# Both key tiles of the first block multiplied together, chunk by chunk, in the opening of a two-block transformer kernel

## The reference, cut to what matters

```python
h = rms_norm(x, swa_norm)                      # per row: x * rsqrt(mean(x*x) + 1e-6) * gain
q, k, v, gate = split(h @ w_in, [2048, 2304, 2560])   # q 2048 wide, k 256, v 256, gate 2048
k = rms_norm(k.reshape(seq, 4, 64), k_gain)    # each of the 4 key heads normalised over its 64 values
v = v.reshape(seq, 4, 64)
...
# sliding-window attention of 32 query heads over the 4 key/value heads, with a bias by distance
# and a sink; gate with silu; output projection; residual. Then a second block with 16 meta tokens.
```

## Time and profile before

| | us |
|---|---|
| median of 3 runs | 1802.08 (1800.97 to 1802.23) |
| the profiled execution's own time | 1800.38 |
| its span | 1798.7 |
| PE busy (matmul) | 1758.5, 98% |
| DVE busy | 1066.0, 59% |
| ACT busy | 912.5, 51% |

### The profile page before, as it was taken

One profiled execution on the slowest core, in us unless ns is written; L12 is line 12 of the kernel. 1 busy time (PEld: TensorE's weight loads), 2 busy tenths in 40 slices (PEclk: granted clock), 3 DMA queues, 4 the chain that ended last, 5 costly groups with the idle time before them and its releaser, 6 DMA issues.

```text
span 1798.7 us, 28913 instructions
## 1 busy us (share of the span) xinstructions
PE 1758.5 (98%) x10281; PEld 1525.7 (85%) x10281; DVE 1066.0 (59%) x2443; ACT 912.5 (51%) x2010; POOL 54.1 (3%) x81
## 2 busy tenths in 40 slices
PE   6999999999999999999999999999999999989899
PEld 5788888888877888898888988889888898877898
DVE  5466767676675334565645546465564655666876
ACT  4466656666574224444545455454544545454443
POOL 1000000000001000000000000000000000000000
PEclk9999999999999999999999999999999999999999
DMA  6433333333325444331322222222222222223441
GB/s 196 126 92 107 98 94 106 92 98 100 91 82 139 135 134 129 103 91 52 95 83 73 82 68 80 84 66 82 72 83 82 73 82 73 79 75 108 159 149 53
DMA packets 283942, 173.85 MB, mean 97 GB/s; under 512 B 16176, under 2 KB 272368, under 8 KB 283840
## 3 DMA queue, kind: packets, MB, share of 16 engines
q1 hardware_dynamic: 267136, 151.08, 28.8%
q0 software_dynamic: 15632, 20.56, 4.9%
q10 hardware_dynamic: 1088, 1.08, 0.3%
HBM read 156.86 MB, written 14.66 MB: 95 GB/s over the span
## 4 chain that ended last, share of the span: by engine, by line
PE 77%; DVE 9%; ACT 6%; issue 3%; ACTq 2%; DMA 1%; DVEq 0%; SPq 0%
PE G L640 63%; PE G L935 3%; ACTq L1506 2%; PE S L1021 1%; DVE wsum L2342 1%; ACT wh L1186 1%; PE O L1039 1%; DVE wl L2350 1%; DVE wl L1741 1%; PE G L752 1%; DMA raw<-in_swa_w_in 1%; PE S L742 1%; PE G L766 1%; PE S L741 1%; ACT wh L1695 1%
## 5 line engine op out<-in xcount | busy, mean ns | idle before, releaser
L640 PE MATMUL G<-xh,wh 128*128 128x512 f32 (+1 forms) x2432 | 792.1, 360 | 3.9 <-DVE xl L1758 2.0
L640 PE MATMUL G<-xl,wh 128*128 128x512 f32 (+1 forms) x2432 | 765.4, 349 | 0.0
L640 PE MATMUL G<-xh,wl 128*128 128x512 f32 (+1 forms) x2432 | 763.0, 348 | 0.0
L640 PEld LDWEIGHTS G<-xh,wh 128*128 128x128 f32 x2432 | 426.6, 189 | 64.9 <-issue 4.8
L640 PEld LDWEIGHTS G<-xh,wl 128*128 128x128 f32 x2432 | 423.6, 188 | 60.9
L640 PEld LDWEIGHTS G<-xl,wh 128*128 128x128 f32 x2432 | 423.9, 188 | 51.2 <-issue 2.6
L1741 DVE TENSOR_TENSOR wl<-raw,wh 128x512 fp32r<-128x512 f32 x472 | 319.4, 688 | 248.4 <-ACT wh L1186 246.0
L1186 ACT ACTIVATE wh<-raw 128x512 fp32r<-128x512 f32 x472 | 284.1, 620 | 16.5 <-PE G L640 8.2
L1563 ACT ACTIVATE att<-att,st 128x144 f32<-128x144 f32 (+3 forms) x64 | 36.9, 577 | 119.8 <-DVE wmeta L2195 68.5
L1289 ACT ACTIVATE p<-S,rq 128x256 f32<-128x256 f32 (+1 forms) x128 | 50.1, 444 | 44.7 <-PE S L742 43.2
L1299 ACT ACTIVATE p<-p,st 128x257 f32<-128x257 f32 (+1 forms) x128 | 60.6, 482 | 0.0
(11 more groups left out here) (316 smaller groups left out, 2312.6 us busy)
## 6 DMA issues: line engine op xcount, KB each, us to landing
raw<-in_w_in SPq DMA_DIRECT2D x112, 512.0 KB, 4.0
raw<-in_swa_w_in SPq DMA_DIRECT2D x68, 512.0 KB, 8.8
raw<-in_swa_w_out SPq DMA_DIRECT2D x32, 512.0 KB, 4.3
raw<-in_w_in POOLq DMA_DIRECT2D x8, 1024.0 KB, 8.1
raw<-in_w_out SPq DMA_DIRECT2D x6, 1024.0 KB, 6.9
spare<-in_w_out SPq DMA_DIRECT2D x6, 1024.0 KB, 6.5
rel_rows<-mixed POOLq DMA_DIRECT2D x16, 383.0 KB, 19.5
mixed<-in_x SPq DMA_DIRECT2D x4, 1024.0 KB, 13.5
```

Of the source, the lines that this page charges most:

```text
L640: mm = pe.matmul(d, w[:, slot, k, :], v[:, k, a:b], start=(first and n == 0), stop=(last and n == 2))
```

## The change

The two key tiles are multiplied together: for each chunk, three matmuls for tile 0 and three for tile 1. The row factors are placed after chunk 13 of both tiles. ACT and DVE split a quarter of both tiles' weights before the four chunks of x of that quarter. The high parts of the first value tile's weights are copied by ACT right after the exponential of the row factors, a quarter at a time as the key tiles leave the buffer (new semaphore `keys_done`). Both key norm chains run beside the first value tile: the key statistics stand after its chunks 5 and 13. The first value tile's load waits for four quarters of low parts, which are now quarters 0 and 1 of both key tiles. Two pairs of semaphores are merged.

```diff
@@ SP: value_weights @@
-                sp.wait_ge(w_lo, 4 + 2 * (g - 1))
+                sp.wait_ge(w_lo, 4 * (g - 1))
@@ PE @@
+            def key_tiles():
+                for k in range(KC):
+                    next_chunk(k)
+                    for g in range(KV // 2):
+                        if k % QTR == 0:
+                            pe.wait_ge(w_lo, 2 * (k // QTR) + g + 1)
+                        product([G[:, g, :]], g, k, PLAIN, k == 0, k == KC - 1, keys_done if g else None)
+                    if k == KC - 3:
+                        first_factors()
...
-            for g in range(KV):
+            key_tiles()
+            for g in range(KV // 2, KV):
                 def at_point(p, g=g):
-                    if g == 1 and p == 3:
-                        first_factors()
-                    if 0 < g <= KV // 2 and p == 5:
-                        key_stat(g - 1)
-                    if g > KV // 2 and p == 5:
+                    if g == KV // 2 and p in (2, 6):
+                        key_stat(p // 4)
+                    if g > KV // 2 and p == 3:
                         value_transpose(g - 1)
-                if g == 1:
-                    pe.wait_ge(x_lo, KC)
-                gemm(T_KV + g, g % 2, [G[:, g, :]], PLAIN, at_point, next_chunk if g == 0 else None)
+                if g == KV - 1:
+                    pe.wait_ge(kv_act, 2)
+                gemm(T_KV + g, g % 2, [G[:, g, :]], PLAIN, at_point)
@@ ACT @@
             for quarter in range(4):
                 key_split_weights(0, quarter)
+                key_split_weights(1, quarter)
...
-            key_split_weights(1, 0)
-            key_split_weights(1, 1)
             row_sum(0)
-            key_split_weights(1, 2)
             act.wait_ge(sq_act, 1)
             row_sum(1)
-            key_split_weights(1, 3)
...
+            def first_value_split(quarter):
+                if quarter == 0:
+                    act.wait_ge(raw_in[0], 16)
+                if quarter < 3:
+                    act.wait_ge(keys_done, QTR * quarter + QTR)
+                else:
+                    act.wait_ge(tile_done, 1)
+                q = slice(QTR * quarter, QTR * quarter + QTR)
+                A(wh[:, 0, q, :], raw[:, 0, q, :], ACT.Copy).then_inc(w_hi, 1)
+            for quarter in range(3):
+                first_value_split(quarter)
+            act.wait_ge(first_mm, 2)
             A(rs1[:, :], O[:, :], ACT.Copy).then_inc(rs1_ok, 1)
+            first_value_split(3)
...
-            for g in range(1, KV):
+            for g in range(KV // 2, KV):
                 for m in range(POINTS):
-                    if m == 4 and g <= KV // 2:
-                        key_square(g - 1)
-                    if m == 6 and g <= KV // 2:
-                        key_rstd(g - 1)
+                    if g == KV // 2 and m in (1, 5):
+                        key_square(m // 4)
+                    if g == KV // 2 and m in (3, 7):
+                        key_rstd(m // 4)
+                    if (g, m) in ((KV // 2, 4), (KV - 1, 0)):
+                        key_split(g - KV // 2)
                     if m % 2 == 0:
                         split((g + 1) // 2, (g + 1) % 2, m // 2, kv_loaded(g + 1))
-                    if m == 7:
-                        key_split(g - 1) if g <= KV // 2 else value_high(0)
+                    if g == KV - 1 and m == 4:
+                        value_high(0)
@@ DVE @@
             for quarter in range(4):
                 key_split_weights(0, quarter)
+                key_split_weights(1, quarter)
                 for c in range(4 * quarter, 4 * quarter + 4):
                     x_lo_of(c)
-            key_split_weights(1, 0)
-            key_split_weights(1, 1)
             row_sum(2)
-            key_split_weights(1, 2)
             dve.wait_ge(sq_dve, 1)
             row_sum(3)
-            key_split_weights(1, 3)
...
-            for g in range(1, KV):
+            for quarter in range(4):
+                split(1, 0, quarter)
+            for g in range(KV // 2, KV):
                 for m in range(POINTS):
-                    if m == 3:
-                        kv_evict(g - 1)
-                    if m == 7:
-                        if g <= KV // 2:
-                            key_finish(g - 1)
-                            key_split(g - 1)
-                        else:
-                            value_rows(0)
+                    if (g, m) == (KV // 2, 0):
+                        kv_evict(0)
+                    if (g, m) == (KV // 2, 4):
+                        key_finish(0)
+                        kv_evict(1)
+                        key_split(0)
+                    if (g, m) == (KV - 1, 0):
+                        key_finish(1)
+                        kv_evict(2)
+                        key_split(1)
+                    if (g, m) == (KV - 1, 5):
+                        value_rows(0)
                     if m % 2 == 0:
                         split((g + 1) // 2, (g + 1) % 2, m // 2)
```

More of the change, by code:

```diff
@@ L239, in build @@
         w_hi, w_lo, tile_done = sem("w_hi"), sem("w_lo"), sem("tile_done")
-        sq_act, sq_dve, rs_done, diag_ok, rs1_mm, rs1_ok = (
-            sem(n) for n in ("sq_act", "sq_dve", "rs_done", "diag_ok", "rs1_mm", "rs1_ok"))
-        gain_in, gain_t, gain_ok = sem("gain_in"), sem("gain_t"), sem("gain_ok")
+        sq_act, sq_dve, rs_done, diag_ok, rs1_ok = (
+            sem(n) for n in ("sq_act", "sq_dve", "rs_done", "diag_ok", "rs1_ok"))
+        gain_in, first_mm, gain_ok = sem("gain_in"), sem("first_mm"), sem("gain_ok")
         t_done, x_hi, x_lo = sem("t_done"), sem("x_hi"), sem("x_lo")
@@ L284, in build @@
         t_sum, s_sum = sem("t_sum"), sem("s_sum")
+        keys_done = sem("keys_done")
         df_hi, df_lo = sem("df_hi"), sem("df_lo")
@@ L680, in _ @@
             pe.wait_ge(gain_in, 16 * 2)
-            pe.transpose(T[:, 0:2 * KC], gain_rows, ident[0:2 * KC, 0:2 * KC]).then_inc(gain_t, 1)
+            pe.transpose(T[:, 0:2 * KC], gain_rows, ident[0:2 * KC, 0:2 * KC]).then_inc(first_mm, 1)
             for c in range(4):
@@ L690, in first_factors @@
                     mm = pe.matmul(O[:, P * t:P * t + P], ones, diag[:, t, :], start=True, stop=True)
-                mm.then_inc(rs1_mm, 1)
+                mm.then_inc(first_mm, 1)
                 pe.wait_ge(gain_ok, 1)
@@ L1220, in _ @@
             A(rstd[:, 0, 0:NB], rstd[:, 0, 0:NB], ACT.Exp, scale=-0.5).then_inc(rs_done, 1)
-            act.wait_ge(rs1_mm, 1)
+            def first_value_split(quarter):
[10 more added lines that the diff above has]
+            act.wait_ge(first_mm, 2)
             A(rs1[:, :], O[:, :], ACT.Copy).then_inc(rs1_ok, 1)
+            first_value_split(3)
             def key_square(c):
@@ L1760, in x_lo_of @@
                                        op1=ALU.subtract).then_inc(x_lo, 1)
-            dve.wait_ge(gain_t, 1)
+            dve.wait_ge(first_mm, 1)
             V.tensor_copy(gnorm[:, :, :].rearrange("p n c -> p (n c)"), T[:, 0:2 * KC]).then_inc(gain_ok, 1)
             def key_split_weights(g, quarter):
-                dve.wait_ge(w_hi, 4 * g + quarter + 1)
+                dve.wait_ge(w_hi, 2 * quarter + g + 1)
                 q = slice(QTR * quarter, QTR * quarter + QTR)
```

## The result

| | before | changed |
|---|---|---|
| median of 6 runs | 1802.15 us | 1808.89 us (1805.65 to 1809.58) |
| ratio | | 1.0034, 95% interval 1.0023 to 1.0045 |
| profiled execution, its own time | 1800.38 us | 1805.65 us |
| its span | 1798.7 us | 1804.0 us |

The change made the kernel 6.7 us (0.34%) slower; between the two profiled executions it is 5.3 us. The trace is of the fastest of the six executions.

The account below looks back on a forecast made before the run. PE, busy 98% of the span, was taken to bound the kernel; -0.7 + 3.85 + 2.0 + 0.3 = +5.45 us gave a forecast median of 1807.5 us, own range 1806.2 to 1809.0, wider range 1804.6 to 1810.2.

Parts of the forecast that it names:

- The hole: PE's 4.2 us wait for the second load: chunk 0's three extra matmuls fit inside it, -0.7 us.
- The chunks: Key-tile chunks: PE takes 1.84 us per chunk instead of 1.14, work moved forward, and PE still sets the pace.
- Rival A: Key-tile chunks supplied, not paced by PE; period grows to less than 1.84 us; 1801.2 us at unchanged period; 5%.
- The wait for the row factors: After chunk 13 of both key tiles: PE stands 5.0 us for the factors against 1.15, +3.85 us.
- The clock behind it: After the row-factor wait: the granted clock falls and slows the following work, +2.0 us, bounds 0 and 2.9.
- The clock in the opening: Behind the wait for the second load: the lower clock until 20.1 us stays as before, no change counted.
- Rival C: Chunk 0's extra work in the hole holds the clock up, shrinking the loss by 1.35 us: 1806.1 us; 7%.
- The key norms: Over the first value tile: PE waits 0.7 us at the second key statistic, +0.3 us net, bounds -0.4 and +2.0.
- The loads, POOL and SP: Value-tile load issued at about 19.3, bias write and unit loads later but with time in hand: 0 us.
- Rival B: Behind the row-factor wait the clock stays up over the 5.0 us: +3.45 us, 1805.5 us; 10%.
- E: Rival: no effect, the lost time is slack somewhere later in the kernel: 1802.1 us; 5%.
- D: Rival: dearer, the clock costs 2.9 us and the key norm chain 2.0: +8.0 us, 1810.1 us; 8%.

Follow-up runs that it names:

- late: Changed kernel with the row factors placed after chunk 15 of the key tiles instead of chunk 13: 1806.76 us, ratio 1.0024.
- early: Changed kernel with row sums, logarithm, exponential and diagonal matrices put among the x chunks on ACT and DVE: 1799.80 us, ratio 0.9991.
- one-number kernels: Kernel before the change, with the row factors after chunk 1 of tile 1 instead of chunk 7: 1809.04 us, ratio 1.0039.
- The kernel with the filled wait: Changed kernel with 20 extra matmuls, results unused, on PE just ahead of the row-factor wait: 1805.38 us, ratio 1.0018.
- the second trace: Changed kernel unaltered, executed and traced again on another chip: 1807.93 us, where the kernel before took 1802.48 us once.
- third trace: Changed kernel unaltered, executed and traced once more on that other chip: 1807.19 us, where the kernel before took 1802.48 us once.
- The trace with the hole filled and the row sums early: Changed kernel with row sums among the x chunks, plus transposes two chunks ahead instead of three: 1797.07 us, ratio 0.9975.

## Why the prediction was right

The forecast was 1807.5 us, the result 1808.89, inside the range. Term by term, against the profiled execution:

- **The hole, -0.7 us.** Right in kind. The six matmuls of chunk 0 ran from 13.42 to 16.15, inside the wait, and the load's landing at 17.4 did not move. They began 1.15 us later than chunk 0 before (12.27), not 0.6; the hole covers that too.
- **The chunks.** Period 1.83 us (28.70 to 37.88 is five of them, 1.84 each), forecast 1.84. Rival A is excluded: PE sets the pace.
- **The wait for the row factors, +3.85 us.** The main term, and right: PE came 40.93 - 37.72 = 3.2 us after the start of chunk 15's transposes (forecast 3.2), the factors 45.95 - 37.72 = 8.2 us after it (forecast 8.2). The late, early and one-number kernels each moved this wait as the account says.
- **The clock behind it, +2.0 us.** The term that was mis-sized. It was 3.7 us in the trace: the factor matmuls took 49.38 - 45.95 = 3.4 instead of 1.84 us, and until 54.0 each matmul took 0.427 instead of 0.232 us, some 2.1 us more. In all three traces of the changed kernel the low clock lasted 10.2 us, and only the first 0.9 to 2.2 us of it fell into the wait, where it is free. Both stretches I had drawn on were shorter, 6.8 us in all, and in the first of them 4.1 us lay in the wait. The kernel with the filled wait puts the price at 3.5 us by the medians and 3.7 by the traces. I took the middle of two rows and gave a price above the larger of them, 2.9, no room. Why it was 10.2 us here and 6.8 behind the 5.2 us wait made in the kernel before stays open.
- **The clock in the opening, 0.** I let the low clock behind the load stay. In the profiled execution it was gone, worth 1.1 us (chunk 15's transposes came at 37.72, not 38.9); in the second trace it was there and longer. Rival C's event so came about in the traced execution, but the extra work alone does not decide it: with the same six matmuls in the hole, two of the seven such traces have the higher clock at 18.5 us and five the lower until 20.5 to 22.7.
- **The key norms, +0.3 us.** Forecast a wait of 0.7 for the second statistic, found 0.63 by starts (65.60 - 64.97) against 0.28 before: +0.35. The chain from 58.55 to 65.60 is 7.05 us, forecast 7.0 to 7.1.
- **The loads, POOL and SP, 0.** The value tile's load was issued at 19.44 (forecast 19.3), and no wait for it appears.

The sum with the measured terms: -0.7 - 1.1 + 3.87 + 3.7 + 0.35 = +6.1 us, against 6.1 at the milestone. Rival B is excluded by the clock and by the filled wait; E by the time. D's clock price, 2.9, was nearer than the forecast's 2.0, but its key norms, +2.0, did not appear.

That the forecast of +5.45 for the profiled execution came out at +5.3 is in part luck. The clock behind the factor wait was 1.7 us dearer than forecast, and the clock in the opening (1.1) and late in the kernel (0.8), neither of them forecast, gave as much back. The medians, which lack that luck, differ by 6.7 us. The 1.4 us between the two differences is of the size of the clock's scatter in the second and third trace; more than that was not shown.

The Trainium skill ("TensorE: Matmul & The Clock Gate", section "Wait — 56ns, not 53.3ns?") gives 215.7 ns between matmuls of 512 columns, by which the change would have uncovered an estimated 5.2 us. This trace again has 1.40 / 6 = 233 ns, and 5.6 us.

## What to carry to other kernels

Before moving work ahead of a wait, ask what the awaited chain starts with. Here it starts with PE's own last transposes and then runs on the other engines for 8.2 us, so what counts is how much of PE's work lies behind those transposes, and interleaving two tiles took 5.6 us of it away. Put such a chain's long steps where its engines idle (the row sums among the x chunks: 9.1 us), and only then fill holes further ahead. A wait of PE costs more than its length: count the low clock that follows, here 3.5 to 3.7 us on a wait of 5.0. And when kernels differ by 1 or 2 us, compare the same stretch of their traces: here the end of the kernel alone varied by 3.4 us between traces.

## What was not expected

- The low clock lasted 10.2 us with a wait of 5.0 us in all three traces of the changed kernel, against 6.8 us with a wait of 5.2 us made in the kernel before, and 6.8 us behind one of 2.1 us.
- In the stretch 13.4 to 16.2 us the table gives 1.00 while the matmuls are 0.427 us apart, the spacing that goes with 0.50 later on. The records of the granted clock start at 16.4 in that trace. The trace with the hole filled and the row sums early gives 1.00 over 13.4 to 17.4 us in the same way, with its matmuls 0.427 us apart. Early in a trace the spacing of the matmuls is the better witness.
- The same program, with an equal factor wait, had its opening 2.1 us longer in one execution than in another.
